# One decoder layer on one core: experts in 12 passes from one sorted list of rows, and two query products placed between short ones

## The reference

```python
h = rms_norm(x, norm1_g)
u, q, kvc, kvs, kvw, g_nsa, g_a, g_b = split(h @ w_in)
glu  = glu_of(s5_scan(u))                  # state-space branch
o    = nsa_attention(q, kvc, kvs, kvw)     # sparse-attention branch
x    = x + (sigmoid(g_a) * (glu @ w_ssm_out) + sigmoid(g_b) * (o @ w_nsa_out)) @ w_o
hf   = rms_norm(x, norm2_g)
gsel = argmax(hf @ w_rg + b_rg)            # one of 4 groups of experts
top_v, top_i = top_k(expert_logits[gsel], 2)
wts  = softmax(top_v) * softmax_weight_of(gsel)
x    = x + sum_e comb[:, e] * (silu(hf @ w_gate[e]) * (hf @ w_up[e])) @ w_down[e]    # 16 experts, inner width 256
x    = x + sigmoid(x @ w_ple_gate) * (p @ w_ple)
y    = rms_norm(x, final_norm_g)
```

## Time and profile before

| | |
|---|---|
| median of 3 runs | 836.08 us |
| the profiled execution | 836.8 us |
| its span in the trace | 835.0 us |
| PE busy | 800.5 us (96%) |
| DVE, ACT, POOL busy | 348.4, 196.6, 140.1 us |
| DMA, mean over the span | 165 GB/s |

### The profile page before, as it was taken

One profiled execution on the slowest core, in us unless ns is written; L12 is line 12 of the kernel. 1 busy time (PEld: TensorE's weight loads), 2 busy tenths in 40 slices (PEclk: granted clock), 3 DMA queues, 4 the chain that ended last, 5 costly groups with the idle time before them and its releaser, 6 DMA issues. The chain is left out here.

```text
span 835.0 us, 13637 instructions
## 1 busy us (share of the span) xinstructions
PE 800.5 (96%) x5101; PEld 520.7 (62%) x5101; DVE 348.4 (42%) x953; ACT 196.6 (24%) x466; POOL 140.1 (17%) x151
## 2 busy tenths in 40 slices
PE   8999999899999999889999999999899999999995
PEld 5465677777778879555566774445675555654441
DVE  3189901555551323766634372115731111024433
ACT  3010201200101453654433100035111111112222
POOL 3049200500002111334500100011210111004000
PEclk9999999999999999999999999999999999999998
DMA  9530494631411497600030476011899999977111
GB/s 325 136 120 0 124 271 148 134 26 50 158 43 55 115 197 218 179 1 1 1 115 2 118 270 249 1 51 64 345 417 395 391 417 419 363 277 263 40 51 38
DMA packets 81509, 137.54 MB, mean 165 GB/s; under 512 B 33958, under 2 KB 57578, under 8 KB 77234
## 3 DMA queue, kind: packets, MB, share of 16 engines
q1 hardware_dynamic: 64636, 110.17, 40.1%
q0 software_dynamic: 3872, 13.90, 4.8%
q10 hardware_dynamic: 12942, 12.64, 4.5%
HBM read 117.08 MB, written 21.72 MB: 166 GB/s over the span
## 5 line engine op out<-in xcount | busy, mean ns | idle before, releaser
L1146 PE MATMUL ps<-hT,w_slot 128*128 128x288 f32 x640 | 155.7, 406 | 0.0
L1146 PEld LDWEIGHTS ps<-hT,w_slot 128*128 128x128 f32 x640 | 121.4, 190 | 34.1 <-issue 0.6
L1146 PE MATMUL ps<-w_slot,hT 128*128 128x512 f32 (+1 forms) x320 | 127.1, 555 | 0.6 <-DMA w_slot<-in_w_in 0.3
L1146 PEld LDWEIGHTS ps<-w_slot,hT 128*128 128x128 f32 x320 | 60.0, 190 | 61.5 <-issue 42.4
L1146 PE MATMUL ps<-w_slot,merged 128*128 128x512 f32 x128 | 56.0, 594 | 1.1 <-DVE merged L2108 1.1
L2572 DVE SCALAR_TENSOR_TENSOR th<-th,ps 128x256 f32<-128x256 f32 x13 | 5.5, 421 | 114.0 <-ACT th L2035 114.0
L1637 PE MATMUL ps<-wgu,hT 128*32 128x256 f32 x480 | 42.6, 380 | 0.0
L1146 PEld LDWEIGHTS ps<-w_slot,merged 128*128 128x128 f32 x128 | 23.9, 190 | 29.9 <-issue 28.2
L1625 PE MATMUL ps<-w_slot,hT 128*128 128x256 f32 x160 | 35.8, 382 | 0.0
L1625 PEld LDWEIGHTS ps<-w_slot,hT 128*128 128x128 f32 x160 | 30.1, 190 | 7.7 <-issue 3.8
L1146 PE MATMUL ps<-qg,w_slot 128*128 128x288 f32 x128 | 33.7, 408 | 0.0
(11 more groups left out here) (445 smaller groups left out, 1246.7 us busy)
## 6 DMA issues: line engine op xcount, KB each, us to landing
merged<-in_w_exp_down SPq DMA_DIRECT2D x11, 1024.0 KB, 13.0
w_slot<-in_w_in SPq DMA_DIRECT2D x8, 1024.0 KB, 7.0
wgu<-in_w_exp_gate SPq DMA_DIRECT2D x8, 1024.0 KB, 12.3
wgu<-in_w_exp_up SPq DMA_DIRECT2D x8, 1024.0 KB, 14.9
w_slot<-in_w_exp_gate SPq DMA_DIRECT2D x8, 1024.0 KB, 13.6
w_slot<-in_w_exp_up SPq DMA_DIRECT2D x8, 1024.0 KB, 16.1
expert_rows<-onsaT ACTq DMA_DIRECT2D x13, 512.0 KB, 8.1
w_slot<-in_w_exp_down SPq DMA_DIRECT2D x5, 1024.0 KB, 15.0
```

What stands on the lines that cost most here:

```text
L1146: ins = pe.matmul(out, a, b, start=(n == 0), stop=(n == len(pairs) - 1))
```

## The change

**Experts.** There are 12 passes. Places are now called columns, and `RANK_OF_COLUMN` gives the rank by count that a column takes. Only expert 0 has a fixed column. Five columns hold up to 128 rows, six 96 and five 64; seven passes have two experts, one of them (pass 10) with 64 partitions each. The orders of the weight loads follow from the new tables. SP loads only expert 0's gate and up parts ahead of the order, and its down part is issued before the wait for the order.

**List.** The first list now covers all experts: `ids` has 16 columns for each half instead of 2. DVE makes expert 0's rows at once (`first_made`), orders the 16 columns (`by_columns`, 16 x 16 elements), and PE moves the rows of second experts to their partitions by small products with the identity (`rows_of_passes`, a new job "list" after two embedding products). The list inside pass 0 goes away, with its work on DVE; DVE works out a row's place in the outputs in pass 0.

**Queries.** The groups ("q", 0, 0) and ("q", 0, 1) move from behind `d` to before `vt` and between `k` and `d`, on PE and on ACT.

```diff
-PLACES_OF_PASS = [[0], [1], [2], [7, 13], [8, 13], [3], [9, 14], [10, 14], [4], [11, 15], [12, 15], [5], [6]]
-NPASS = len(PLACES_OF_PASS)
-LOADED = [0, 1, 2, 7, 13, 8, 3, 9, 14, 10, 4, 11, 15, 12, 5, 6]
-LAST_PASS = [max(n for n, places in enumerate(PLACES_OF_PASS) if place in places) for place in LOADED]
+RANK_OF_COLUMN = [0, 1, 5, 6, 2, 7, 8, 3, 9, 10, 14, 4, 11, 12, 13, 15]
+COLUMNS_OF_PASS = [[0], [1], [2, 12], [3, 12], [4], [5, 13], [6, 13], [7], [8, 14], [9, 14], [10, 15], [11]]
+NPASS = len(COLUMNS_OF_PASS)
+OF_PARITY = [-(-NPASS // 2), NPASS // 2]
+LOADED = [0, 1, 2, 12, 3, 4, 5, 13, 6, 7, 8, 14, 9, 10, 15, 11]
+LAST_PASS = [max(n for n, columns in enumerate(COLUMNS_OF_PASS) if column in columns) for column in LOADED]
 NX = 4
-DOWN_SLOT = [0, 1, 2, 0, 1, 2, 0, 2, 1, 0, 2, 0, 1, 2, 0, 1]
+DOWN_SLOT = [l % 3 for l in range(NE)]
...
-    loads = [LOADED.index(place) for place in PLACES_OF_PASS[n]]
-    return [loads[0]] * 3 + [loads[-1]]
+    loads = [LOADED.index(column) for column in COLUMNS_OF_PASS[n]]
+    own = 2 if COLUMNS_OF_PASS[n][-1] == NE - 1 else 3
+    return [loads[0]] * own + [loads[-1]] * (4 - own)
...
-    return steps + [("pp",) + job for job in PP_JOBS[1 + 1:len(PP_JOBS) - PP_LEFT]]
+    steps += [("pp",) + job for job in PP_JOBS[2:4]] + [("list", 0, 0)]
+    return steps + [("pp",) + job for job in PP_JOBS[4:len(PP_JOBS) - PP_LEFT]]
...
-            for u in range(2):
-                load_gate_up(u, u)
+            load_gate_up(0, 0)
...
             load_weights("ple")
             sp.wait_ge(pe_done, PLAN.done(("wo", NT - 2, 1)))
+            load_down(0, 0)
             sp.wait_ge(order_made, 1)
-            at_place = {0: 0, 1: 1}
+            at_column = {0: 0}
...
-            load_down(0, 0)
-            read_place(2)
-            load_gate_up(2, expert(2))
-            load_down(1, 1)
...
+            for l in range(1, NX):
+                read_column(l)
+                load_gate_up(l, expert(l))
+            load_down(1, expert(1))
             load_down(2, expert(2))
-            read_place(3)
-            load_gate_up(3, expert(3))
-            for l in range(4, NE):
-                read_place(l)
+            for l in range(NX, NE):
...
+            base_at, cap_at, split_at, first_at, rank_of = (place_tables[:, i] for i in range(5))
+
+            def row_of(out, first, step):
+                pool.iota(out, [[step, out.shape[-1]]], base=first, channel_multiplier=0, allow_small_or_imprecise_dtypes=True)
+            row_of(base_at[:, 0:NPASS], 0, CAP)
+            row_of(base_at[:, 12:15], 2 * CAP + 96, 3 * CAP)
+            pool.memset(base_at[:, 15:16], float(10 * CAP + 64))
+            for at, cap in ((slice(0, 2), 128), (slice(2, 4), 96), (slice(4, 5), 128), (slice(5, 7), 96), (slice(7, 8), 128),
+                            (slice(8, 10), 96), (slice(10, 11), 64), (slice(11, 12), 128), (slice(12, 16), 64)):
...
-            pool.wait_ge(*emptied(("first",)))
-            for u in range(2):
-                gather_rows(u, u)
+            pool.wait_ge(first_made, 1)
+            gather_rows(0, 0)
+            pool.wait_ge(*emptied(("list",)))
+            gather_rows(1, 1)
...
-                pool.wait_ge(list_made, j + 1)
...
+            def query_products(m, h):
+                wq = wk("q", 512)[:, :, P * m:P * m + P]
+                o = begin(("q", m, h))
+                finish(product(o[:, 0:HALF], [(wq[:, k], hT[:, k, HALF * h:HALF * h + HALF]) for k in range(KD)]))
+            pe.wait_ge(*w_need["q"])
+            query_products(0, 0)
...
+            query_products(0, 1)
...
-            pe.wait_ge(*w_need["q"])
-            for m in range(GQA):
-                wq = wk("q", 512)[:, :, P * m:P * m + P]
+            for m in range(1, GQA):
                 for h in range(2):
-                    o = begin(("q", m, h))
-                    finish(product(o[:, 0:HALF], [(wq[:, k], hT[:, k, HALF * h:HALF * h + HALF]) for k in range(KD)]))
+                    query_products(m, h)
             for m in range(KD_A, KD):
                 gate_products(m)
...
+            def rows_of_passes(out):
+
+                pe.matmul(out[:, 0:NPASS], ident[:], by_column[:, 0:NPASS], start=True, stop=True)
+                for h in range(2):
+                    pe.matmul(out[96:P, 2 + h:9 + h:3], ident[:, 32 * h:32 * h + 32], by_column[:, 12:15], start=True, stop=True)
+                return pe.matmul(out[64:P, 10:11], ident[:, 0:64], by_column[:, 15:16], start=True, stop=True)
...
+                elif what == "list":
+                    pe.wait_ge(columns_made, 1)
+                    finish(rows_of_passes(begin(("list",))))
...
-                gate_up(j, 0, 0, lambda: turn_rows(j, 1, 1, 0),
-                        lambda: list_by_slot(ps[:, RING], j * 4 + 2, ids, NPASS).then_inc(list_done, 1))
+                gate_up(j, 0, 0, lambda: turn_rows(j, 1, 1, 0))
...
-                    if n == 1:
-                        pe.wait_ge(list_made, j + 1)
...
-            link(dve.tensor_copy(first_f[:, 0:2], o[:, 0:2]))
-            empty(tt(idx[:, 0:2], first_f[:, 0:2], o[:, 2:4], ALU.add))
+            link(dve.tensor_copy(first_f[:], o[:, 0:NE]))
+            tt(idx[:, 0:1], first_f[:, 0:1], o[:, NE:NE + 1], ALU.add).then_inc(first_made, 1)
             link(dve.tensor_reduce(place_e, more, axis=X, op=ALU.add))
-            link(dve.scalar_tensor_tensor(is_at, place_e.unsqueeze(2).broadcast_to(n_ef), float(P), ebase[:].unsqueeze(1).broadcast_to(n_ef),
-                                          ALU.mult, ALU.is_equal))
+            empty(tt(by_rank[:], first_f[:], o[:, NE:2 * NE], ALU.add))
...
+            dve.wait_ge(*emptied(("first",)))
+            link(by_columns())
+            dve.tensor_reduce(by_column[:], more, axis=X, op=ALU.add).then_inc(columns_made, 1)
+            dve.wait_ge(columns_made, 1)
+            link(tt(more, is_at, cap_at.unsqueeze(1).broadcast_to(n_ef), ALU.mult))
+            link(dve.tensor_reduce(cap_e, more, axis=X, op=ALU.add))
...
+            o = take(("list",))
+            empty(dve.tensor_copy(idx[:, 1:NPASS], o[:, 1:NPASS]))
...
-            split_c, cap_c, base_c, row0_c, pass_c = (by_choice[:, i] for i in range(5))
-            link(tt(both, sel[:], kind_e.unsqueeze(1).unsqueeze(1).broadcast_to(n3), ALU.mult))
-            link(dve.tensor_reduce(base[:], both, axis=X, op=ALU.add))
-            dve.tensor_scalar(split_c, base[:], 2.0, None, ALU.is_ge)
-            dve.tensor_scalar(cap_c, base[:], -32.0, float(CAP), ALU.mult, ALU.add)
-            link(tt(both, sel[:], pass_e.unsqueeze(1).unsqueeze(1).broadcast_to(n3), ALU.mult))
-            link(dve.tensor_reduce(pass_c, both, axis=X, op=ALU.add))
-            dve.scalar_tensor_tensor(row0_c, split_c, 96.0, rank[:], ALU.mult, ALU.add)
-            link(dve.scalar_tensor_tensor(base_c, split_c, 96.0, pass_c, ALU.mult, ALU.add))
+            cap_c, base_c, split_c = (by_choice[:, i] for i in range(3))
...
+                for i, of_expert in enumerate((cap_e, base_e, split_e)):
+                    ins = tt(of_choice[:, i], sel[:], of_expert.unsqueeze(1).unsqueeze(1).broadcast_to(n3), ALU.mult)
+                place_link(j, ins, 1)
+                for i in range(3):
+                    ins = dve.tensor_reduce(by_choice[:, i], of_choice[:, i], axis=X, op=ALU.add)
+                place_link(j, ins, 2)
...
-                place_link(j, tt(at_pass[:], of_pass.unsqueeze(3).broadcast_to([P, 2, NT, NPASS]),
-                                 ebase[:, 0:NPASS].unsqueeze(1).unsqueeze(1).broadcast_to([P, 2, NT, NPASS]), ALU.is_equal), 3)
...
-                rows_at_slots(row)
...
-                dve.wait_ge(list_done, j + 1)
-                place_link(j, dve.tensor_copy(first_f[:, 0:NPASS], ps[:, RING, 0:NPASS]), 5)
-                tt(idx[:, 2:NPASS], first_f[:, 2:NPASS], ps[:, RING, NPASS + 2:2 * NPASS], ALU.add).then_inc(list_made, 1)
```

More of the change, by code:

```diff
@@ L1611, in weights_there, with gate_up @@
                     pe.wait_ge(gu_ld[l % NX], j * 128 + 32 * (l // NX + 1))
-            def gate_up(j, n, u, between=None, late=None):
+            def gate_up(j, n, u, between=None):
                 weights_there(j, n)
@@ L1879, in _, with take_query @@
                 copy(None, xg[:, 7 * i:7 * i + 7].rearrange("p g n -> p (g n)"), o[:, 0:7 * NCH])
+            def take_query(m, h):
+                o = take(("q", m, h))
+                empty(act.activation(qT[:, m, HALF * h:HALF * h + HALF], o[:, 0:HALF], ACT.Copy, scale=SCALE))
+            take_query(0, 0)
             for i in range(0, 8, 2):
@@ L2016, in _ @@
                 p = TILES[t]
-                if what == "pp" and (t, c) == (1, 1):
-                    act.wait_ge(lg_made, 1)
-                    act.activation(r16[:, :, 0:5], r16[:, :, 0:5], ACT.Exp).then_inc(lg_exp, 1)
                 if what == "pT":
```

134 lines of the change are left out of this document (73 added, 61 removed).

## The result

| | before | changed |
|---|---|---|
| median, first comparison | 836.39 us (835.44 to 837.02, 4 runs) | 827.63 us (824.68 to 828.95, 4 runs) |
| ratio | | 0.9877 [0.9851, 0.9904] |
| the same kernels again, other chip time | 838.18 us (834.07 to 842.90, 11 runs) | 826.04 us (825.00 to 829.99, 7 runs) |
| ratio | | 0.9849 [0.9817, 0.9880] |
| profiled execution, span | 836.8, 835.0 us | 828.95, 827.2 us |

Faster by 1.2 to 1.5%, with 827.63 where 826.9 was forecast. Only fast executions enter the ratios; one slow run, 1191.39 us in experiment 3, is left out. The ratio is the comparison's own estimate and not the quotient of the two medians, which by themselves give 8.8 and 12.1 us.

What follows compares the result with a forecast made beforehand. The prediction took DMA weight loads, not PE alone, to bound the expert stage. Queries -2.9, experts -6.8 and tail +0.5 gave -9.2 us against the profiled 836.8; from the 0.7 lower median it forecast 826.9, range 821.5 to 831.5.

Steps and rivals of the forecast that it cites:

- Which resource bounds the stage: Expert stage: DMA bytes limit the gain to 6.8 us, where PE alone would gain 13.8.
- load 14 as the point to reckon with: Last pass but one (pass 10): it needs load 14, the second expert's weights, which PE alone would reach at 709.0.
- the rival with PE as the bound: Expert stage: the DMA engines keep up, so -13.8 - 2.9, near 819.4 us; chance 0.12, with cases halfway to it.
- I take 716.0: Expert stage: load 14 lands at 716.0, between 717.0 at 404 GB/s and 712.7 at 418, so 6.8 us gained.
- The slow rival: Expert stage: the rate stays at 370 GB/s, load 14 lands at 728.9, total 839.8 us; chance 0.07.
- The list: Start of the experts: a new 1.1 us wait for pass 1's rows cancels an old one; 0.7 us gained in sum.
- the cover of 1.37 us: State-space stage: the first moved query group, 3.9 us, fills PE's whole 1.37 us wait ahead of the second part of `vt`.
- The gap: In `k`: PE's 2.84 us idle time after 126 of 128 instructions, read as running out of code; 1.5 us gained.
- half of the block is long work: In `k`: some 34 instructions ahead move the code block's boundary earlier; 1.5 us of the gap gained, 1.3 left.
- Nothing saturated beside them: State-space stage: PE's idle times of 1.37 and 2.84 us were said to have no full resource beside them.
- The rival that nothing of the gap is won: Queries: code fetch mostly hidden, so only 1.4 us gained, total 828.4 us; within the weaker cases, chance 0.17 together.
- The tail: After the last pass but one: its store shares with loads standing closer together, costing +0.5 us (0 to 1.5).

Runs made afterwards that it cites:

- experiment 3: The kernel before with only the second query group moved, between `k` and `d`: ratio 1.0002 [0.9981, 1.0023].
- Experiment 7: The changed kernel loading only half the columns of each down part from load 3 on, all products still made: 0.9757, 818.44 us.
- experiment 5: The changed kernel with expert 1 fixed to column 1 and its gate and up parts loaded ahead of the router: 0.9818, 824.17 us.
- experiment 6: The kernel of experiment 5 with pass 1's rows from the first list (early rows): 0.9805, 822.84 us; then expert 1's down part also early: 0.9801, 821.49 us.
- experiment 4: The kernel before with 16 repeats of the last short transpose of `x` put ahead of `vt`: ratio 0.9946 [0.9930, 0.9963].
- experiment 2: The kernel before with only the first query group moved, ahead of `vt`: 0.9914 [0.9891, 0.9938], 831.65 us.
- experiment 8: The changed kernel with its last load, 2.1 MB of embedding weights, held back until the last down products are done: 0.9856, 827.11 us.
- experiment 1: The kernel before with both query groups moved as in the change, and nothing else: 0.9919 [0.9895, 0.9942], 832.11 us.
- experiment 9: The changed kernel with the queries back where the kernel before has them, so experts and list alone: 0.9934, 833.75 us.
- variant of experiment 8: The kernel of experiment 6 with early rows, its last load held back too: 0.9814 [0.9783, 0.9845], 823.52 us.

## Why the prediction was right, and where it was not

*Which resource bounds the stage*: right. The forecast was 52.2 MB behind the order, load 14 as the point to reckon with, and waits of 5 to 8 us; there were 52.29 MB, load 14 landed last before pass 10, and the waits were 4.95 us plus 1.14 for the rows. Experiment 7, with fewer bytes and the same products, has none of these waits: the bytes are the cause, and they are why the rival with PE as the bound failed. The Trainium skill (Perfetto Trace Analysis, Engine Utilization) has about 435 GB/s as the bound of one core; 413 over the whole and 418 in the best long stretches were measured, so 819.4 was out of reach for this many bytes. The term's size was off: 8.3 us for 6.8. "I take 716.0, nearer the mean, because ... SP's waits for free slots ... stay" was the wrong step: with a fuller queue they don't stay, and the mean rose from 404 to 413 GB/s over the stretch, 416 where 370 had been. The slow rival rested on that 370; by experiments 5 and 6 it is the rate when loads are ahead and slots are full, not what the engines can do.

*The list*: right on the new wait, 1.14 us for 1.1. DVE's part ahead of the first transposes was to be equal; the wait that it ends fell from 1.24 to 0.15 us, which paid for the new list products.

*Queries*: the cover of 1.37 us, right. The gap was taken as 1.5 won and 1.3 left; all 2.84 went, and the term was 4.2 for 2.9 in the profile. The step that failed is "half of the block is long work": what counts is the delay of PE against the time at which the code is there (experiment 4). "Nothing saturated beside them" was misread too: from 146 to 151, up to where the gap begins, the DMA engines had a share of 1.06 to 1.16. The second group, which was to cover the next block in `d`, had nothing to cover: experiments 2 and 3. The rival that nothing of the gap is won is refuted by experiment 2. The Trainium skill (Runtime: NRT & Kernel Launch, Instruction fetch mechanics) has such crossings mostly hidden; at this place 2.84 to 3.66 us stand in view, and they move with a count of instructions.

*The tail*: wrong. +0.5 (0 to 1.5) was forecast, +4.7 came in the profile, and with it the range of that term failed. The 19.8 us from store to PE had been just enough before, and now they were 22.3. Experiments 7 and 8 put that down to the loads beside them: with the last load held back the gather took 8.4 us for 10.3, and with half down parts the wait was gone. The wait of 2.2 us then cost 1.7 more by the clock, which no term had. An idle time of PE ahead of full work can cost more than itself, but didn't in every execution (last section).

*The sum*: -9.2 forecast, -4.2 - 8.3 + 4.7 = -7.8 in the profile; the terms missed by 1.3 and 1.5 one way and 4.2 the other. The comparisons of runs give 10.3 (8.0 to 12.5) and 12.7 (10.1 to 15.3) us (8.8 and 12.1 by the medians), so the change is worth more than its profile shows, by 1 to 5 us. Experiments 1 and 4 have an excess of 2 to 3 us, experiment 3 none, so it goes with moving PE's instructions ahead of `k`. Most of it is the clock, which the prediction nowhere had: the kernels with the gap of some 3 us (before, experiments 3 and 9) ran at a mean of 0.992, those without it or with 1.01 us of it (the changed kernel in the second comparison, experiments 1, 2 and 4) at 0.994 to 0.995, an estimated 1.9 us. The four runs of the first comparison had 0.992 all the same, and there the gain was smaller. The profiles of experiments 3 and 9 show half clock right behind the gap, and the one of before happened not to have it. That all of the clock's difference arises at this place isn't shown, since only one execution of each kernel has a timeline. That 827.63 lay so near to 826.9 is in part luck: the terms' errors cancelled, and the change's effect on the clock was in none.

## What to carry to other kernels

When PE and the DMA engines are both full, reckon each pass twice, by work and by bytes up to the last load that a pass needs, and read a dip in GB/s beside full slots as reserve and not as the rate to expect. Loading earlier pays only as far as slots can hold it. A gap named "issue" that stands at a fixed count of instructions is moved or filled by other work put ahead of it; before believing a neat account of what fills it, move one piece at a time. And before reading a difference of a few microseconds between two profiles, compare the mean granted clock of each profiled execution with those of the other runs of its kernel.

## What was not expected of the hardware

The code gap: 2.4 to 2.8 us lie between the transfer of 0.02 MB on the instruction queue and PE's going on, in four kernels. The gap's length in view was 2.84, 2.99 and 3.66 us at the same place in three of them, and the longest goes with the latest transfer (151.6 for 150.8).

The clock: after a wait of 2.22 us PE's next four products took 3.27 us for 1.88, 2.93 in the second profiled execution (wait of 2.53) and 3.40 in experiment 5 (wait of 2.47). The granted clock also fell behind idle times of 1.93, 2.99 and 3.66 us (variant of experiment 8, experiments 3 and 9). After waits of 0.46 and 1.25 us (experiment 8, and experiment 6 with early rows), of 1.64 us (variant of experiment 8) and of 2.84 us (the kernel before) it stayed at 1.00. So it did in experiment 9 after the longest wait for tile 0 of all:

```profile
753.10 1.25 PE L1765 MATMUL ps<-ident,x 128*128 128x128 f32 x8 [2.60 <-DVE x L2136]
754.18 1.88 PE L1163 MATMUL ps<-w_slot,kv 128*128 128x512 f32 x4
```

The length of a wait alone, then, doesn't tell whether PE loses its clock: 1.93 us was enough once, and 2.84 us wasn't another time.
